# Later conditioning vectors summed by VectorE from buffers of their own, and two stage ends taken tile by tile, in a two-layer hybrid trunk

## The reference

```python
c_act = jax.nn.silu(c)                                # 1024 numbers
for layer in range(2):
    mod = c_act @ cond_w[layer] + cond_b[layer]       # 6 * 1024 numbers
    sh_m, sc_m, g_m, sh_f, sc_f, g_f = jnp.split(mod, 6, axis=-1)
    h = x * (1.0 + sc_m) + sh_m
    y = even_mixer(h) if layer == 0 else retention_mixer(h)
    x = layer_norm(ALPHA * x + g_m * y, ln_w[layer, 0], ln_b[layer, 0])
    h = x * (1.0 + sc_f) + sh_f
    y = swiglu(h) if layer == 0 else moe_swiglu(h)     # 8 experts, top 2
    x = layer_norm(ALPHA * x + g_f * y, ln_w[layer, 1], ln_b[layer, 1])
```

## Time and profile before

| | |
|---|---|
| median of 3 runs | 1742.06 us (1741.53 to 1742.91) |
| the profiled execution | 1742.85 us, span 1740.9 us, mean granted clock 0.966 |
| mixer of layer 0 behind its input products | 131 to 266 us of the span |
| first stage end, PE idle but for the turns | 293 to 310 us |
| dense feed-forward | 310 to 506 us |
| second stage end | 506 to 525 us |
| retention stage | 525 to 728 us |
| routing and experts | 728 to 1715 us |

### The profile page before, as it was taken

The page is one execution under the profiler, slowest core; times in us unless marked ns, Lnnn a source line. Parts: engine busy times, 40 slices in busy tenths (PEclk is TensorE's granted clock), DMA queues, the critical chain, the costliest instruction groups (busy, mean ns, idle before and its releaser), DMA issues.

```text
span 1740.9 us, 20082 instructions
## 1 busy us (share of the span) xinstructions
PE 1617.3 (93%) x7810; PEld 1297.4 (75%) x7810; DVE 1282.3 (74%) x1160; ACT 1009.3 (58%) x867; POOL 132.8 (8%) x94
## 2 busy tenths in 40 slices
PE   4888996999969999879999999999999999999996
PEld 1874765787858777658888888888888888888875
DVE  1374536655456665688889888898898898988986
ACT  1432223444434444347777777777777777777775
POOL 0421310000000100220000000000000000000005
PEclk8898998999989999979999999999999999999998
DMA  9347885855454543539999999999999999999993
GB/s 329 130 167 283 322 316 193 285 183 185 169 169 146 164 171 145 187 129 391 388 379 390 375 388 387 369 388 379 376 389 375 381 388 371 384 385 367 385 382 151
DMA packets 234370, 515.33 MB, mean 296 GB/s; under 512 B 8936, under 2 KB 40960, under 8 KB 234176
## 3 DMA queue, kind: packets, MB, share of 16 engines
q1 hardware_dynamic: 228272, 491.99, 77.3%
q10 hardware_dynamic: 2992, 11.79, 1.9%
q0 software_dynamic: 3008, 10.20, 1.9%
HBM read 507.15 MB, written 13.11 MB: 299 GB/s over the span
## 4 chain that ended last, share of the span: by engine, by line
PE 86%; DVE 7%; issue 2%; ACT 2%; DMA 2%; POOL 1%; DVEq 0%; SPq 0%; ACTq 0%; POOLq 0%
PE bank L762 25%; PE bank L764 25%; PE bank L763 25%; PE bank L741 2%; PE bank L925 2%; DMA ring<-in_cond_w 2%; PE bank L1185 1%; PE bank L757 1%; DVE arena L1768 1%; DVE small L1689 1%; PE bank L774 0%; ACT w_part L1310 0%; DVE w_part L1643 0%; DVE hs L1715 0%; PE bank L1167 0%
## 5 line engine op out<-in xcount | busy, mean ns | idle before, releaser
L1654 DVE TENSOR_TENSOR w_lo<-ring,w_hi 128x2048 fp32r<-128x2048 f32 x336 | 764.7, 2290 | 104.1 <-ACT w_hi L1537 102.2
L1537 ACT ACTIVATE w_hi<-ring 128x2048 fp32r<-128x2048 f32 x334 | 640.5, 1918 | 196.3 <-PE bank L764 187.0
L762 PE MATMUL bank<-w_lo,heT_hi 128*128 128x512 f32 x896 | 353.8, 395 | 3.8 <-DVE w_lo L1654 2.2
L764 PE MATMUL bank<-w_hi,heT_hi 128*128 128x512 f32 x896 | 349.7, 390 | 0.0
L763 PE MATMUL bank<-w_hi,heT_lo 128*128 128x512 f32 x896 | 348.9, 389 | 0.0
L1643 DVE TENSOR_TENSOR w_part<-ring,w_part 128x1024 fp32r<-128x1024 f32 x148 | 183.4, 1246 | 211.0 <-ACT w_part L1310 206.2
L1310 ACT ACTIVATE w_part<-ring 128x1024 fp32r<-128x1024 f32 (+1 forms) x162 | 169.1, 1049 | 252.0 <-PE bank L764 247.3
L762 PEld LDWEIGHTS bank<-w_lo,heT_hi 128*128 128x128 f32 x896 | 168.3, 188 | 39.0 <-issue 5.9
L764 PEld LDWEIGHTS bank<-w_hi,heT_hi 128*128 128x128 f32 x896 | 168.2, 188 | 35.9
L763 PEld LDWEIGHTS bank<-w_hi,heT_lo 128*128 128x128 f32 x896 | 168.5, 188 | 33.6
L762 PE MATMUL bank<-w_part,hT_hi 128*128 128x512 f32 (+1 forms) x448 | 179.8, 401 | 14.2 <-DVE w_part L1643 13.1
(11 more groups left out here) (344 smaller groups left out, 1586.8 us busy)
## 6 DMA issues: line engine op xcount, KB each, us to landing
ring<-in_moe_w_up SPq DMA_DIRECT2D x224, 1024.0 KB, 8.8
ring<-in_moe_w_down SPq DMA_DIRECT2D x112, 1024.0 KB, 7.8
ring<-in_cond_w SPq DMA_DIRECT2D x24, 2048.0 KB, 9.1
ring<-in_ffn_w_up SPq DMA_DIRECT2D x22, 1024.0 KB, 8.2
ring<-in_od_w_in SPq DMA_DIRECT2D x8, 2048.0 KB, 7.9
ring<-in_ev_w_in SPq DMA_DIRECT2D x5, 2048.0 KB, 12.4
ring<-in_ffn_w_down SPq DMA_DIRECT2D x5, 2048.0 KB, 7.7
ring<-in_od_w_in SPq DMA_DIRECT2D x8, 1024.0 KB, 8.0
```

Of the source, the lines that this page charges most:

```text
L762: mm(bank, lhs[0], rhs[1], start=start, stop=False)
L764: return mm(bank, lhs[0], rhs[0], start=False, stop=stop)
L1537: f(w_hi[:, n % 3], half_landed(act, it, u, half), ACT.Copy) \
L1654: tt(w_lo[:, buf], at, w_hi[:, buf].bitcast(F32), ALU.subtract).then_inc(S["w_lo"], 1)
```

## The change

Ten units, four plus six, still go through the ring and the row steps. The last fourteen, `SUM_COND` = (0, 10), (0, 11) and all of layer 1, do not:

- **Loads.** SP fetches each as 8 chunks of 128x512 (256 KB) into `chunks`, five buffers; four chunks stand ahead of each weight load from `ffn_up` 3 on, and a chunk waits for the sum of the one five before it.
- **Sums.** Behind each split of a part, DVE runs `sum_cond`: none, one or two multiply-adds `acc += chunk * c` (after: L1708), four for a weight unit, from `ffn_up` 1 to the last `od_g`: 112 in all. Each of the 14 begins with the bias row written out by one TENSOR_SCALAR (after: L1704).
- **Broadcasts.** PE multiplies `acc` by a matrix of ones (`SPREAD_AT`): four in the feed-forward's upper part, three in its lower part, five in the retention stage, two behind the router.
- **Order.** The broadcasts of (0, 6) to (0, 9) (`MIX_COND`) stand behind the turn of the mixed rows. Only (0, 4) and (0, 5) stay in the solve, behind level 2.
- **Stage ends.** In the first two, each tile is modulated, turned and split by itself; PE multiplies tile 0 with three parts between the two turns; DVE's splits of the next parts stand between its steps, ahead of the `affine` pairs.
The core of the diff:

```diff
-COND_BATCHES = (tuple((0, u) for u in FIRST_COND), tuple((0, u) for u in range(4, N_COND)),
-                tuple((1, u) for u in range(N_COND)))
+COND_BATCHES = (tuple((0, u) for u in FIRST_COND), tuple((0, u) for u in range(4, 10)))
+SUM_COND = ((0, 10), (0, 11)) + tuple((1, u) for u in range(N_COND))
...
-LEVEL_COND = {2: (4, 5), 3: (6, 7), 4: (8, 9)}
-UP_COND = {0: (0, 10), 1: (0, 11), 2: (1, 0), 3: (1, 1), 4: (1, 2), 5: (1, 3), 6: (1, 4), 7: (1, 5), 8: (1, 6), 9: (1, 7)}
...
+LEVEL_COND = {2: (4, 5)}
+MIX_COND = (6, 7, 8, 9)
+SPREAD_AT = {
+    ("ffn_up", 3): (0,), ("ffn_up", 5): (1,), ("ffn_up", 7): (2,), ("ffn_up", 9): (3,),
+    ("ffn_down", 1): (4,), ("ffn_down", 3): (5,), ("ffn_down", 5): (6,),
+    ("od_qk", 0): (7,), ("od_g", 0): (8,), ("od_v", 1): (9,), ("od_qk", 2): (10,), ("od_g", 2): (11,),
+    ("router",): (12, 13),
+}
+CHUNKS = 5
...
@@ SP
+                while fetched < KC * len(SUM_COND) and fetched < 4 * (stream_place[key] - 2 - SUM_START) + CHUNKS \
+                        and stream_place[key] >= 2 + SUM_START:
+                    (l, u), k, i = SUM_COND[fetched // KC], fetched % KC, fetched % CHUNKS
+                    if fetched >= CHUNKS:
+                        sp.wait_ge(S["chunk_used"], fetched - CHUNKS + 1)
+                    sp.dma_start(chunks[:, i], cond_w[l, P * k:P * k + P, 512 * u:512 * u + 512]).then_inc(chunk_in[i], 16)
+                    fetched += 1
                 load(s, source(key))
...
@@ ACT
-            cond_kept(2)
             split_to(part_no["ev_out", 0, 0] + BUFS)
+            for u in MIX_COND:
+                cond(0, u)
             for u in range(2):
                 split_ahead("ev_out", u)
-            normalise(0)
-            turned(2, BY_TILE)
+            normalise(0, True)
             for i in range(FILLS):
                 act.dma_start(slots[i * SEQ:(i + 1) * SEQ], x[0]).then_inc(S["slots_out"], 16)
...
@@ DVE
+            def sum_cond(key):
...
+                for _ in range({("ffn_down", 5): (2, 2), ("od_qk", 0): (0, 0, 0, 4)}.get(key[:-1], (1, 0, 1, 2))[key[-1]]):
+                    n, k = sums[0] // KC, sums[0] % KC
...
+                    total = acc[:, n % 2]
+                    if k == 0:
+                        filled(dve, "cond", *(SUM_COND[n - 2] if n > 1 else (0, 9)))
+                        dve.wait_ge(S["sum_bias_in"], 16)
+                        col = N_COND * l + u
+                        V.then(ts(total, sum_bias[:], ident[:, col:col + 1], None, ALU.mult))
+                    else:
+                        dve.wait_ge(S["chunk_used"], sums[0])
+                    dve.wait_ge(chunk_in[sums[0] % CHUNKS], 16 * (sums[0] // CHUNKS) + 16)
+                    stt(total, chunks[:, sums[0] % CHUNKS], cT[:, k:k + 1], total, ALU.mult, ALU.add) \
+                        .then_inc(S["chunk_used"], 1)
+                    sums[0] += 1
...
                 rest_of_residual(0)
                 moments(0)
+                if part_left:
+                    split_to(part_left + 1)
                 to_normalise(stage, 0)
                 rest_of_residual(1)
...
+                if part_left:
+                    modulated(0)
+                    moments(1)
+                    turned(stage + 2, BY_TILE[:2])
+                    to_normalise(stage, 1)
+                    split_to(part_left + 2)
+                    modulated(1)
+                    turned(stage + 2, BY_TILE[2:], 2)
...
+                for t in range(NT):
+                    if part_left:
+                        split_to(part_left + 3 + t)
                     affine(stage, t)
...
@@ POOL
-            G.then(tt(xs[:, 0], xs[:, 0], ln[:, 0], ALU.mult))
-            tt(xs[:, 0], xs[:, 0], ln[:, 1], ALU.add).then_inc(S["first_done"], 1)
...
-    nc = bacc.Bacc("TRN2", target_bir_lowering=False, num_devices=1)
+    nc = bacc.Bacc("TRN2", target_bir_lowering=False, num_devices=1, dynamic_dma_scratch_size=4096)
```

More of the change, by code:

```diff
@@ L753, in cond @@
                 bank, full = to_fill(pe, "cond", l, u)
+                if (l, u) in SUM_COND:
+                    n = SUM_COND.index((l, u))
+                    pe.wait_ge(S["chunk_used"], KC * n + KC)
+                    mm(bank[:], ones, acc[:, n % 2], start=True, stop=True).then_inc(full, 1)
+                    return
                 b = BATCH_OF[l, u]
@@ L785, in part, with project @@
                 return [part_buffer(key, i) for i in range(2)]
-            def project(key, stage, n=512, steps=None):
+            def project(key, stage, n=512, steps=None, second=None):
                 outs = [to_fill(pe, *key, t) for t in range(NT)]
                 for j, t in steps or [(j, t) for j in range(4) for t in range(NT)]:
+                    if second and (j, t) == (0, 1):
+                        second()
                     w = part(*key, j)
@@ L1072, in _ @@
             for u in range(FFN // 256):
-                project(("ffn_up", u), 2, steps=None if u else FIRST)
-                if u - 1 in UP_COND:
-                    cond(*UP_COND[u - 1])
+                project(("ffn_up", u), 2, steps=None if u else FIRST,
+                        second=None if u else lambda: turn(2, h_ready(1), BY_TILE[2:]))
+                spread("ffn_up", u)
                 if u:
@@ L1110, in _ @@
             for h in range(RH):
-                project(("od_qk", h), 3, steps=None if h else FIRST)
-                if h - 1 in OD_COND:
-                    cond(1, OD_COND[h - 1])
+                project(("od_qk", h), 3, steps=None if h else FIRST,
+                        second=None if h else lambda: turn(3, h_ready(2), BY_TILE[2:]))
+                spread("od_qk", h)
                 if h:
@@ L1116, in _ @@
                 project(("od_v", h), 3)
+                spread("od_v", h)
                 for t in range(NT):
@@ L1623, in modulate, with turned @@
                         tt(hs[:, t, cols], hs[:, t, cols], mod[:, a:a + 512], ALU.add).then_inc(S["h_ready"], 1)
-            def turned(stage, order=(0, 1, 2, 3)):
-                for n, i in enumerate(order):
+            def turned(stage, order=(0, 1, 2, 3), first=0):
+                for n, i in enumerate(order, first):
                     half, t = i // 2, i % 2
@@ L1953, in _ @@
             split_to(part_no["ev_out", 0, 0] + BUFS)
[L1954 to L1959 removed]
+            split_ahead("ev_out", 0)
+            for t in range(NT):
+                residual(0, 2, lambda t, half: ("ev_out", half, t), t, (0,))
+            split_to(part_no["ffn_up", 0, 1])
+            stage_end(0, lambda t: residual(0, 2, lambda t, half: ("ev_out", half, t), t, (1,)), 0, 3, part_no["ffn_up", 0, 1])
             def ffn_turned(u):
@@ L2201, in _ @@
             to_normalise(3, 1)
+            affine(3, 0)
             affine(3, 1)
```

125 lines of the change are left out of this document (70 added, 55 removed).

## The result

The changed kernel takes 1746.06 us (median of 20 runs, 1743.61 to 1750.8) against 1742.63 us for the kernel before in runs beside it: a ratio of 1.0023, 95% interval 1.0017 to 1.0029. Forecast were 1722 us and a gain. Its profiled execution is one of the quicker ones (1744.08 us, span 1742.2).

What follows compares the result with a forecast made beforehand. PE, busy for 93% of the span, was taken as the bound; mixer -21.5 and the smaller terms summed to -20.2 us, from 1742.85 to 1722.6, as a median 1722. Its own range was 1716 to 1728, all cases 1711 to 1733.

Steps and rivals of the forecast that it cites:

- The chunks at the first stage end: First stage end: PE starts 6 us earlier, DVE gives back 5.4, -0.6; chunks issued 8 us before most are due.
- the four broadcasts behind the turn: Behind the mixed rows' turn: four at 0.95 us fill PE's 3.58 us wait; taken as 0, bounds -0.5 and +4.
- The mixer: Row steps and broadcasts leaving PE save 22.3 us, less 0.7 to 0.8 lost once ahead of level 2: -21.5.
- the wait ahead of level 2: Mixer solve: PE waits for DVE to free `yay` of level 1 after the scores; 0.7 to 0.8 us lost once.
- the row steps between `kv` and `ws`: Mixer, between the state's steps: two row steps of 1.85 us gone, saving 1.0 and 0.6 as waiting remains.
- The retention stage: Five broadcasts instead of two, +2.6; longer waits for a split at three later heads, 0.7 each, +2.1.
- The second stage end: Tile 1's products start at 523.7 instead of 530.1, but `od_v` of head 0 ends at 549.4, not 547.7: +1.7 us.
- Rival 4: All 28 units: multiply-adds with their waits for chunks become the bound; slower than before, 1746 us or more; chance 0.04.
- Rival 2: Feed-forward and retention stage: DVE late, 28 units at 0.4 us or so, +11, 1733 us; chance 0.20.
- Rival 1: Stage ends pay in full: both keep their 6 us, 12.8 better, 1709 us; chance 0.12.
- Rival 3: Mixer: row steps filled idle time; nine give 0.6 us instead of 1.85, +11, 1733 us; chance 0.08.
- Rival 5: POOL's gathers wait because of the smaller descriptor memory: +15, 1737 us; chance 0.04.

Runs made afterwards that it cites:

- Run 2: Changed kernel with ACT's six fills of `slots` moved, one each behind units 2 to 7 of `ffn_up`: 1730.08 us, 0.9927.
- run 4: Changed kernel with fills moved into `ffn_up` and first five chunks asked two loads sooner, first two stage ends as in the kernel before: 1732.12 us, 0.994.
- run 6: Changed kernel with fills moved into `ffn_up`, first chunks asked sooner, eight idle transposes ahead of the waits of `kv` and `ws` steps but the first: 1723.44 us, 0.9894.
- run 5: Changed kernel, fills in `ffn_up`, six multiply-adds a feed-forward unit, the rest in `od_g`, four chunk buffers, a unit's own load ahead of its chunks: 1753.14 us, 1.0052.
- run 10: Changed kernel with idle transposes in `kv` and `ws`, fills in the retention stage, five multiply-adds a feed-forward unit, eight in each `od_g`: 1718.28 us, 0.9866.
- run 1: Changed kernel with the first five chunks asked for two loads sooner in SP's stream: 1737.15 us, 0.9958.
- run 12: Changed kernel with six multiply-adds a feed-forward unit, four chunk buffers, own load ahead of chunks, and the fills in the retention stage: 1747.82 us, 1.0025.
- run 13: Changed kernel with each fill as two transfers over 256 rows of 512 columns, 2 KB runs, twelve ACT issues: 1744.25 us, 1.0013.
- run 11: Changed kernel with each fill as one transfer of two half-width columns, 2 KB runs, six issues: 1840.03 us, 1.0551.

## Why the prediction was wrong

- **The chunks at the first stage end** (-0.6 forecast, 12.7 us off). The step that failed is the sentence that a unit's chunks are issued 8 us before they are due, and the transfers are at 46 to 55%. Both were read in the middle of the feed-forward. The window 320:360, near its start, stands in the forecast's own rows with a DMA share of 0.97, and in 308:335 of that trace, beside the fills, a load of `ffn_up` took 18.4 us (median) to land, where it took 7.2 in 360:500. The first chunks stand in SP's stream ahead of `ffn_up` 3, whose load waits until `ffn_up` 0 has been split (294.8); that is 3.9 us before DVE wants them, and just there ACT has put 6.3 MB on the same DMA engines. I had the fills in the sum, as 3.83 us of ACT's time, and not as traffic. Run 2 gives 15.6 us back in this stretch of the trace, which is then 2.9 us better than forecast. Of that, 2.2 are the stage end (2.8 us of gain in run 4's comparison, 0.6 forecast). The rest stands ahead of it, at the four broadcasts behind the turn, which were taken as 0: with them the clock is 1.00 when the products of `ev_out` begin (251:255), where it was 0.57 (270:274), and these products end 25.7 us behind the turn instead of 27.2.
- **The mixer** (-21.5 forecast, -17.0 measured). The row steps and broadcasts went at their price, and the wait ahead of level 2 came as forecast (0.94 us for DVE, 0.7 to 0.8 forecast). What failed is the pricing of the row steps between `kv` and `ws` by their own length less the wait that stays: they also kept the clock. Four steps at 2.05 instead of 1.1 us are 3.7; run 6 has the missing 4.4 us.
- **The retention stage** (+4.7 forecast, +7.9 measured). One multiply-add, 0.7 us, at each later head was taken, 2.1 in all; the waits grew by 2.8, at head 1 by 1.5, twice as much. The broadcasts cost less than the 2.6 forecast, since two more and not three stand in the stretch: 1.7. The term that the sum didn't have is the clock. Each window at 0.79 loses 1.7 of its 8 us, and there are three instead of one: 3.4 by my estimate. The three together are 7.9. Runs 5 and 10 give 5 us back.
- **The second stage end** (+1.7 forecast): about 1.5 us worse than forecast. Run 4 shows that the half by half form is a gain of 1.1 there; the wait of 3.31 us is the one that run 10 takes away with the sums at `od_qk` 0.
- **Right, or nearly:** the multiply-add at 0.69 (measured 0.785 over all 112, 14% more), DVE in the feed-forward, the four broadcasts behind the turn (3.92 us for eight products, the high clock, so that the bound of +4 did not come), six fewer broadcasts, the end (0.7).
- **The rivals.** Rival 4 named the right thing, waits for chunks, and the right side, but as a load of all 28 units; it was one wait in one place, and 0.04 was far too little. Rival 2 is a part of the truth in the retention stage. Rival 1 did not come even with the chunks in time: the ends gave 2.8 and 1.1 us, not 6 each. Rivals 3 and 5 did not happen.

Left open: why the changed kernel's twenty runs scatter by 7 us, where the four each of run 6 and run 10 scatter by 1.4 and 2.6. A part of such scatter is the clock: in the traces of runs 1, 5 and 12 it was 0.76 to 0.86 in 170:180, where the others looked at have 1.00, and their mixer took 74.8 us instead of 72.2.

## What to carry to other kernels

A new transfer must be placed against what is in flight when it is asked for, at its first use above all: look at the issues of every queue there, with packets and not only bytes, since here a queue of 65.5 KB packets beside one of 2 KB packets got nearly all the bytes. Before taking filler work off PE, ask what the clock will do in the waits that stay: here 8 idle transposes ahead of each wait were worth 4.4 us, and in the retention stage the fallen clock cost more than the longer waits themselves. Work spread evenly by number isn't even in cost: put it where its engine has no one waiting behind it (`od_g`), not ahead of a rotation that PE waits for.

## What the runs showed of the hardware

- Two DMA queues with unlike packets (65.5 KB against 2 KB): 32 packets each in 3 us, 1.05 MB against 0.07 MB (changed kernel, 305:308). With 2 KB in both: 96 packets against 110 in 1 us, 0.18 MB against 0.20 MB (run 13, 310:311).
- Waits of PE and the clock behind them in the retention stage: 1.24 us twice, clock 1.00 (before); 1.90 us, 0.79 in the 8 us around it, and 2.75 us twice, 0.79 (changed); 2.10 us, 1.00 twice and 0.79 once (run 10). The length of the wait alone doesn't decide it.
- The fills as one transfer of two halves each ran at 51 GB/s (run 11); the same halves as two transfers at 259 (run 13, 290:305), the contiguous ones at 333 with the little else in 288.5:308.
- An issue of a contiguous megabyte took ACT 0.63 us, one of 256 rows of 2 KB 1.1 us (12.07 for eleven).
